# A hybrid attention trunk on one core: the attention items of branches A and B start one projection unit sooner

## What is computed

```python
def hybrid_layer(x, ...):
    h = rms_norm(x, norm_g)
    proj = einsum('bsd,de->bse', h, w_in) + b_in        # all q, k, v, gates of the branches
    y_a = indexer_sparse_attention(a_q, a_k, a_v, i_q, i_k, i_w)
    y_b = chunked_relpos_attention(b_q, b_k, b_v, rel_bias)
    qk = silu(causal_depthwise_conv(concat([c_q, c_k]), conv_w, conv_b))
    y_c = head_layer_norm(mlstm_chunkwise(...), c_norm_w)
    merged = sum over branches of sigmoid(gates) * (y * silu(z)) @ w_branch
    return x + merged @ w_out

# in branch A, per block of 128 queries (t = 0..3):
    logits = einsum('bqhd,bsd->bqhs', iqb, ik)          # 4 index heads: "index"
    score = einsum('bqhs,bqh->bqs', relu(logits), iwb)
    score = where(admissible, score, -inf)
    _, sel = top_k(score, 128)                          # "topk"
    # softmax attention of 8 heads over the selected keys
```

## Time and profile before

| | |
|---|---|
| median of 3 runs | 1283.32 us |
| lowest, highest | 1283.2, 1283.62 us |
| profiled execution, its own time | 1283.52 us |
| its span | 1281.3 us |
| granted clock of TensorE, mean | 0.999 |
| busy: TensorE, VectorE, ScalarE, GpSimd | 99%, 54%, 49%, 47% |
| read from HBM | 111.23 MB, 90 GB/s over the span |

### The profile page before, as it was taken

The page is one execution under the profiler, slowest core; times in us unless marked ns, Lnnn a source line. Parts: engine busy times, 40 slices in busy tenths (PEclk is TensorE's granted clock), DMA queues, the critical chain, the costliest instruction groups (busy, mean ns, idle before and its releaser), DMA issues.

```text
span 1281.3 us, 19785 instructions
## 1 busy us (share of the span) xinstructions
PE 1263.1 (99%) x6486; PEld 1064.3 (83%) x6486; DVE 689.0 (54%) x1432; ACT 633.3 (49%) x1157; POOL 599.5 (47%) x759
## 2 busy tenths in 40 slices
PE   8999999999999999999999999999999999999997
PEld 6788888888988888888888888878888888888887
DVE  6799887745545221123687988785644631121144
ACT  6565676686534332333256466767754433323233
POOL 6654333423235555455775642333322455455463
PEclk9999999999999999999999999999999999999999
DMA  7223111221322323333342321122212222332331
GB/s 296 83 82 115 67 50 58 66 91 51 113 69 70 103 82 98 99 97 108 99 158 89 99 85 65 50 66 73 76 51 102 89 82 82 106 98 90 103 102 66
DMA packets 37047, 116.35 MB, mean 91 GB/s; under 512 B 4080, under 2 KB 4464, under 8 KB 36720
## 3 DMA queue, kind: packets, MB, share of 16 engines
q1 hardware_dynamic: 34672, 111.24, 26.3%
q10 hardware_dynamic: 2304, 4.20, 1.0%
HBM read 111.23 MB, written 4.19 MB: 90 GB/s over the span
## 4 chain that ended last, share of the span: by engine, by line
PE 92%; DVE 4%; ACT 2%; issue 1%; POOL 1%; DMA 0%; ACTq 0%; SPq 0%; DVEq 0%; POOLq 0%
PE acc L653 75%; PE ps_o L812 5%; PE ps_t L799 2%; PE ps_t L790 2%; PE ps_s L768 2%; PE ps_o L819 1%; PE ps_s L774 1%; DVE turn L1371 1%; DVE bk_lo_s L1351 1%; PE ps_s L757 1%; PE acc L686 1%; PE spare L750 1%; PE spare L831 1%; DVE prob L1392 0%; DMA xT<-x 0%
## 5 line engine op out<-in xcount | busy, mean ns | idle before, releaser
L604 POOL TENSOR_TENSOR w_lo<-w_raw,w_hi 128x256 fp32r<-128x256 f32 x744 | 586.0, 817 | 664.2 <-ACT w_hi L889 664.0
L653 PE MATMUL acc<-h_hi,w_hi 128*128 128x512 f32 x1120 | 447.6, 400 | 0.7 <-POOL h_lo L615 0.7
L653 PE MATMUL acc<-h_lo,w_hi 128*128 128x512 f32 x1120 | 438.8, 392 | 0.0
L653 PE MATMUL acc<-h_hi,w_lo 128*128 128x512 f32 x1120 | 292.6, 395 | 0.0
L889 ACT ACTIVATE w_hi<-w_raw 128x1024 fp32r<-128x1024 f32 (+1 forms) x210 | 202.0, 962 | 119.5 <-PE acc L653 90.8
L653 PEld LDWEIGHTS acc<-h_hi,w_hi 128*128 128x128 f32 x1120 | 210.7, 188 | 41.7 <-POOL h_lo L615 1.8
L653 PEld LDWEIGHTS acc<-h_lo,w_hi 128*128 128x128 f32 x1120 | 210.7, 188 | 39.4
L653 PEld LDWEIGHTS acc<-h_hi,w_lo 128*128 128x128 f32 x1120 | 205.6, 188 | 40.4
L1513 DVE SCALAR_TENSOR_TENSOR gated<-prob,acc 128x512 f32<-128x512 f32 x16 | 11.0, 688 | 246.7 <-PE acc L653 246.7
L1131 ACT ACTIVATE prob<-acc,par_half 128x512 f32<-128x512 f32 x48 | 33.1, 690 | 147.1 <-PE acc L653 147.1
L1078 ACT ACTIVATE prob<-prob,neg_max 128x128 f32<-128x128 f32 (+3 forms) x128 | 70.7, 553 | 9.2 <-DVE neg_max L1392 8.9
(11 more groups left out here) (274 smaller groups left out, 1823.0 us busy)
## 6 DMA issues: line engine op xcount, KB each, us to landing
w_raw<-w_full SPq DMA_DIRECT2D x162, 512.0 KB, 3.4
w_raw<-w_mix SPq DMA_DIRECT2D x48, 256.0 KB, 2.6
rel<-rel ACTq DMA_DIRECT2D x16, 256.0 KB, 2.9
xT<-x SPq DMA_DIRECT2D x4, 512.0 KB, 6.2
stage<-x_tok SPq DMA_DIRECT2D x4, 512.0 KB, 10.1
xT<-x SPq DMA_DIRECT2D x1, 2048.0 KB, 9.3
x_kept<-xT SPq DMA_DIRECT2D x1, 2048.0 KB, 9.0
xT<-x_kept SPq DMA_DIRECT2D x1, 2048.0 KB, 8.3
```

Of the source, the lines that this page charges most:

```text
L604: last = pool.tensor_tensor(w_lo[:, slot, part, :], w_raw[:, raw, part, :], w_hi[:, slot, part, :].bitcast(F32), ALU.subtract)
L653: last = pe.matmul(acc[slot][:, :], w[:, slot, k, :], x[:, k, :], start=(place == 0), stop=(place == 3 * nk - 1))
```

## The change

INDEX_AT moves index(3) from after unit 15 to after unit 14 (U_AK is 3), so that its four groups stand in the passes of unit 15 instead of unit 16. ROUNDS loses its last entry, the two rounds after unit 15. The loop of the middle part ends after unit 14 (range(7, 15)), and first is 15, so items start in the passes of unit 16. The items of A and B are spread over units 15 to 36 as u counts them, 22 instead of 21. TWICE gives items 1 and 5 a second top-k round as well, which keeps the total at 48 and has tile 2's mask ready with item 9 and tile 3's with item 23, as before. The two loads rel_bias 0 and 1 stand one unit sooner. What hangs on items (STACK_AT, rel_bias from 2 on, rows 1 to 5) moves with them; what hangs on units (turn_v, conv, z, y_split) stays. No instruction is added or taken away.

```diff
--- before.py
+++ after.py
@@ -65,14 +65,14 @@
 
 
 SPREAD = 16
-INDEX_AT = {U_AK + 7: 2, U_AK + 12: 3}
+INDEX_AT = {U_AK + 7: 2, U_AK + 11: 3}
 STACKS_A = {5: ("ak_hi",), 9: ("ak_lo", "aq_hi"), 10: ("aq_lo",)}
 CUT = ("cut", None)
 
 
 
-ROUNDS = {U_AK + n: 4 if n in (10, 11) else 2 for n in range(4, 13)}
-TWICE = (9, 13)
+ROUNDS = {U_AK + n: 4 if n in (10, 11) else 2 for n in range(4, 12)}
+TWICE = (1, 5, 9, 13)
 
 
 STACK_AT = {}
@@ -144,7 +144,7 @@
     index(1)
 
     work = [("topk", (t, r, r + 1)) for t in (1, 2, 3) for r in range(TOPK // 8)]
-    for u in range(7, 16):
+    for u in range(7, 15):
         units(u, u + 1)
         if u == 7:
             seq.append(("rope", U_AK))
@@ -164,7 +164,7 @@
                 seq.append(work.pop(0))
     seq.append(("rel_bias", 0))
     seq.append(("rel_bias", 1))
-    first = 16
+    first = 15
     n, soon, late, rows = 0, [], [], -1
     for u in range(first, U_BZ):
```

## The result

| | before | after |
|---|---|---|
| median of 8 runs, us | 1283.26 | 1287.12 |
| lowest, highest | 1283.11, 1284.2 | 1286.66, 1287.72 |
| profiled execution's span | 1281.3 | 1285.0 |

The changed kernel is slower: +3.86 us, a ratio of 1.0029 with a 95% interval of 1.002 to 1.0038. The forecast was 1288.0, within 1284.0 to 1291.5. The kernel before was timed again beside it, hence its 8 runs.

A forecast was written before the change was run, and what follows sets the result against it. TensorE, busy 99% of the span, was taken as the bound, so only its standing time counts. Early +2.0 and later +0.3 us a layer, over two layers +4.6 on 1283.4, gave 1288.0 us, range 1284.0 to 1291.5.

The forecast's parts named there:

- Step 6: Items 5 to 8: values 4 in item 7 waits 0.35 us for the division to free ps_o; 0 if aq_lo 1 takes 1.39.
- Step 7: Units 26 to 33: waits move to items 41, 42 and 45, +0.3 us a layer, bounds -3.4 and +1.5.
- Steps 1 and 2: TensorE's own matmuls and interruptions cost 0; everything up to 103.28, where tile 1's mask is written, is unchanged.
- Step 3: Up to item 0: scores 0 at 111.6 on VectorE, 108.07 on TensorE; VectorE 3.5 us behind instead of 1.0.
- Step 4: Items 0 to 2: turn_p 0 waits 1.17 us against 0.27 before; exp table load hidden, otherwise 1.28 more a layer.
- Step 5: Item 4: exp 2 only at 117.4, so turn_p 2 is 0.5 us late and values 1 waits 0.2.
- Step 8: Work moving along on queues: two rel DMAs on ScalarE, SP's loads and GpSimd's splits cost 0; unit 18's load wanted at 121.9.
- nothing to measure: Rival: early cost 1.2 a layer and later waits 0.5 less, +1.4 us in all, 1284.8; chance 0.15.
- Faster: Rival: meetings in units 26 to 33 come apart, their 3.4 us a layer go; -4.4 us, 1279; chance 0.06.
- Lag and table: Rival: exp table load falls behind the early wait and later waits reach their bound; +9.6 us, 1293; chance 0.08.
- clock: Rival: a stop drops TensorE's clock, one unit a layer at half clock, 2 x 5.44 us on top, 1298.9; chance 0.01.

The follow-up runs named there:

- (1): Kernel before, items unmoved, with two more top-k rounds of VectorE ahead of item 0 and one round with each later item: 1286.33 us, ratio 1.0023.
- (2): Changed kernel with no round of tile 2 ahead of item 0 and eight later items carrying two rounds: 1283.62 us, ratio 1.0001.
- experiment 5: Changed kernel with each rel_bias DMA issue from 2 on one item later: 1283.92 us, ratio 1.0004.
- experiment 4: Kernel before with each rel_bias DMA issue from 2 on one item later: 1278.32 us, ratio 0.9957.

## Why the prediction was right

The mechanism was the one forecast, and the runs show it from both sides: the lag alone brings the cost (1), and the change without the lag costs nothing that can be measured (2). Of the forecast 4.6 us 3.86 came: early +1.6 a layer for +2.0, late +0.2 for +0.3. The size is in part luck, since in steps 6 and 7 errors cancel. Point by point:

- **Steps 1 and 2** hold: equal counts; VectorE's index(3) after starts at 103.44, which is 103.28 and the 0.16 of the later start of the program.
- **Step 3** holds to 0.1: scores 0 on VectorE at 111.77 (111.6 forecast), on TensorE at 108.23 (108.07).
- **Step 4** holds: 1.16 for 1.17. The split was not foreseen: 0.71 for the bank of scores 0 and 0.45 for the exp. The table load was not in it, as ScalarE's timeline after shows:

```profile
109.01 1.28 ACT L1078 ACT_TABLE_LOAD   x1
112.10 0.40 ACT L1078 ACTIVATE prob<-prob,neg_max 128x128 f32<-128x128 f32 x1 [1.81 <-DVE neg_max L1392]
...
116.27 1.06 ACT L889 ACTIVATE w_hi<-w_raw 128x1024 fp32r<-128x1024 f32 x1 [0.17 <-ACT bk L964]
117.23 0.39 ACT L1078 ACTIVATE prob<-prob,neg_max 128x128 f32<-128x128 f32 x1
```

The load ends at 110.29, ahead of the maximum for which the exp waits until 112.10. The bound of 1.28 more was not reached, nor was any pause behind the load to be seen.
- **Step 5** was mis-sized: 0.13 at item 4, not 0.7. exp 2 came at 117.23, where 117.4 was forecast and the program's later start would make 117.56. The last two rows show why: it starts 0.10 before the recorded end of the copy ahead of it (116.27 + 1.06 = 117.33). Laying ScalarE's durations end to end, as the prediction did, adds such tenths: from exp 1 (113.56, where 113.4 and the later start had it) to exp 2 the chain came out 0.33 shorter. turn_p 2 was hardly late then, and the 0.2 of values 1 never arose. The Trainium skill (ScalarE: Activation LUTs, "What ACT_TABLE_LOAD costs") gives about 93 ns for the overlap of instructions that follow each other; the rows agree with 0.10.
- **Step 6** held in size (0.29 for 0.35 at item 7) by two errors that cancel. aq_lo 1 took 1.39, not 2.0, and the prediction gave 0 for that case. But TensorE, hardly held in step 5, came to item 7 at 124.83 where 125.16 was laid out, so it met the division all the same. Nor did the lag stop costing there: item 11 waits 0.27, again for the division (VectorE's record of it starts at 135.03), and none was forecast behind item 7. With step 5 the early sum is +1.6 instead of +2.0.
- **Step 7** had the sum, +0.3 against +0.2, and part of the reason wrong, so that its size is luck: the waits were laid out at items 41, 42 and 45 and came at 37, 40, 41, 42 and 44, and the one of 1.23 at item 37 was not forecast. The clash at item 35 was to dissolve. It does not; ScalarE's timeline after has

```profile
220.32 0.33 ACTq L1072 DMA_DIRECT2D rel<-rel  x1
220.70 0.72 ACT L1078 ACTIVATE prob<-prob,neg_max 128x512 f32<-128x512 f32 x1 [3.51 <-DVE neg_max L1392]
...
233.75 0.63 ACT L1059 ACTIVATE z_tanh<-turn 128x512 f32<-128x512 f32 x1 [4.20 <-DVE neg_max L1392]
```

and VectorE's at the same places

```profile
216.50 0.78 DVE L1465 TENSOR_TENSOR norm<-i_iw_row,decay 4x128 f32<-4x128 f32 x1
217.31 1.10 DVE L1467 TENSOR_TENSOR decay<-decay,run_max 4x512 f32<-4x512 f32 x1
218.46 1.10 DVE L1371 SCALAR_TENSOR_TENSOR turn<-pad,par,turn 128x512 f32<-128x512 f32 x1
219.59 0.69 DVE L1392 CUSTOM_DVE_ANT_0 prob<-ps_s,rel 128x512 f32<-128x512 f32 x1
...
234.41 0.69 DVE L1377 SCALAR_TENSOR_TENSOR ck<-z_tanh,turn 128x512 f32<-128x512 f32 x1 [1.08 <-ACT z_tanh L1059]
```

At item 35 the tanh no longer stands behind the DMA issue, as laid out. But a rows step and a conv lie ahead of scores 35 on VectorE, and ScalarE does nothing for 3.51 us, with exp 35 behind the issue. exp 35 needs scores 35 anyway, so the issue costs it only the 0.38 from 220.32 to 220.70: experiment 5, which takes the issue away, shortens the wait in item 37 by 0.37 and leaves 0.86 of it to VectorE's queue. That meeting of rows, conv and scores ahead of item 35 is what the layout missed. The second clash, at item 39 (4.20, with conv_gate 6 waiting 1.08), is the one forecast. What the prediction did not see at all is the size of the hold in the kernel before: its working prices it through conv_gate's tanh, 1.08 once, while moving the issue by one item takes 2.5 us a layer off before and 1.6 off after (4 and 5).
- **Step 8** holds: the two rel DMAs cost nothing at their new place, and unit 18 starts at 121.57 (121.9 forecast).

Of the rivals, *nothing to measure* is not what happened, though the interval's lower end lies on its bound. *Faster* would have needed the later waits to go: experiment 4 shows that they can, but by the place of rel_bias, which the change leaves alone. *Lag and table* and the *clock* didn't come: the granted clock is 1.00 in both windows above, through the stops at items 2 and 7, and also from 210 to 250 us. The prediction took the warning of the Trainium skill (TensorE: Matmul & The Clock Gate, "HAM oscillation") as a rule by which this rival's price was due. That was read too widely: the case described there has pauses longer than any stop here, and none of these stops brought the lower level.

Why the lag's cost ends with item 11 was not tried by itself: that it does is read from starts alone.

## What to carry to other kernels

Before work is pulled forward on the bounding engine, compare how much each engine loses ahead of that point: a follower that falls behind by more than its buffers cover (here more than 2.3 us, which was nearly free, and less than 3.6, which cost 3.0, with two score banks and items 1.4 to 1.6 us apart) stops the leader, though their totals are the same. Lay out the order by starts, since a row's idle time shows only part of a wait. And look in each engine's queue for a DMA issue that waits: everything behind it stands still, and issuing it one item later was worth more here (5 us) than the change at stake.

## What the runs showed of the hardware

**VectorE beside GpSimd.** GpSimd's timeline, the split of before at aq_lo 1, and then that of after:

```profile
121.40 3.72 POOL L604 TENSOR_TENSOR w_lo<-w_raw,w_hi 128x256 fp32r<-128x256 f32 x4 [4.23 <-ACT w_hi L889]
```

```profile
117.41 2.81 POOL L604 TENSOR_TENSOR w_lo<-w_raw,w_hi 128x256 fp32r<-128x256 f32 x4 [5.52 <-ACT w_hi L889]
```

Before, aq_lo 1 (122.53 for 2.00) lies inside a split, and both are long: four splits take 3.72 instead of 2.81, aq_lo 2.00 instead of 1.39. After, GpSimd is idle when aq_lo 1 runs at 120.33, and both are short. The other such steps of the kernel before bear it out: of its 64 (L1339, L1345, L1351, one instruction each), the 28 that meet no split take 0.67 to 0.69 us, the 36 that meet one 0.69 to 1.20. The length of these steps therefore depends on what they meet, and I had taken it over as fixed. The Trainium skill (SBUF — State Buffer, "Who interferes with whom") says that a VectorE instruction with two SBUF inputs contends with a GpSimd instruction that reads SBUF, and calls the port pair that they share an exclusive lock. The rows agree that this pair collides; one after the other the six instructions would end at 121.40 + 2.81 + 1.39 = 125.60, and they end at 125.12, so they overlap by about 0.5 us in the records.

**The table load runs ahead of its activation's wait.** It starts at 109.01, while the exp that needs it waits for VectorE until 112.10. A table is thus loaded in idle time where the activation waits, and costs something only where the exp would otherwise be ready: 0.27 a layer before.
